# Tile 1's gated outputs in two banks, with the state products in half rows of the array

## What is computed

```python
    q_dec = q * jnp.exp(b)
    k_inv = k * jnp.exp(-b)
    a = jnp.where(causal, jnp.einsum('bhncd,bhnsd->bhncs', q_dec, k_inv), 0.0)
    o_intra = jnp.einsum('bhncs,bhnsv->bhncv', a, v)
    ...
    o_inter = jnp.einsum('bhncd,bhndv->bhncv', q_dec, s_prev)
    return (o_intra + o_inter).reshape(B, H, S, dv)
    ...
    o_gla = rms_norm(o_gla.transpose(0, 2, 1, 3), gla_out_gain[l])
    o_gla = (o_gla * jax.nn.silu(gr.reshape(...))).reshape(B, S, GLA_V)
```

## Time and profile before

| what | value |
|---|---|
| median of 3 runs | 301.67 us (301.47 to 302.24) |
| the profiled execution | 301.75 us, of which the span from first to last instruction is 300.0 us |
| mean granted clock of TensorE | 0.996 of full speed |
| PE busy | 292.4 us (97%) |
| DVE busy | 242.4 us (81%) |
| ACT busy | 171.6 us (57%) |
| DMA | 55.45 MB, mean 185 GB/s |

### The profile page before, as it was taken

One profiled execution on the slowest core, in us unless ns is written; L12 is line 12 of the kernel. 1 busy time (PEld: TensorE's weight loads), 2 busy tenths in 40 slices (PEclk: granted clock), 3 DMA queues, 4 the chain that ended last, 5 costly groups with the idle time before them and its releaser, 6 DMA issues.

```text
span 300.0 us, 4026 instructions
## 1 busy us (share of the span) xinstructions
PE 292.4 (97%) x1373; PEld 243.3 (81%) x1373; DVE 242.4 (81%) x403; ACT 171.6 (57%) x242; POOL 19.1 (6%) x41
## 2 busy tenths in 40 slices
PE   7999999999999999999999999999999999999992
PEld 7788888788898888887888888888888888888881
DVE  1999999977879687988888888889897978787155
ACT  2898999969765897717170808080808080813123
POOL 5050100000021001300000000000000000000011
PEclk9999999999999999999999999999999999999998
DMA  7987836737867121392929292929291929030003
GB/s 235 364 289 266 263 119 251 218 131 264 298 190 227 53 92 70 95 329 90 331 82 336 79 343 69 346 66 352 63 363 47 367 54 366 25 120 0 0 0 140
DMA packets 37318, 55.45 MB, mean 185 GB/s; under 512 B 2950, under 2 KB 26554, under 8 KB 37306
## 3 DMA queue, kind: packets, MB, share of 16 engines
q1 hardware_dynamic: 37140, 55.13, 54.4%
q10 hardware_dynamic: 166, 0.17, 0.2%
HBM read 53.72 MB, written 1.57 MB: 184 GB/s over the span
## 4 chain that ended last, share of the span: by engine, by line
PE 94%; DMA 2%; DVE 1%; issue 1%; POOL 1%; ACT 0%; SPq 0%; POOLq 0%; DVEq 0%
PE acc L508 15%; PE acc L510 15%; PE acc L509 15%; PE aux L508 13%; PE aux L509 13%; PE aux L510 13%; DMA raw<-in_w_in 2%; PE aux L613 1%; PE acc L562 1%; PE acc L565 1%; PE acc L568 1%; PE aux L683 1%; DVE x_sb L1366 1%; PE aux L707 1%; PE aux L665 1%
## 5 line engine op out<-in xcount | busy, mean ns | idle before, releaser
L1137 DVE TENSOR_TENSOR w_lo<-raw,w_hi 128x2048 fp32r<-128x2048 f32 x47 | 105.6, 2286 | 14.5 <-ACT w_hi L877 14.4
L877 ACT CAST w_hi<-raw 128x2048 fp32r<-128x2048 f32 x47 | 87.9, 1908 | 4.4 <-DMA raw<-in_w_ffn_up 2.1
L508 PE MATMUL aux<-w_hi,aT_hi 128*128 128x512 f32 (+1 forms) x180 | 69.8, 388 | 0.0
L509 PE MATMUL aux<-w_lo,aT_hi 128*128 128x512 f32 (+1 forms) x180 | 69.7, 387 | 0.0
L510 PE MATMUL aux<-w_hi,aT_lo 128*128 128x512 f32 (+1 forms) x180 | 69.7, 387 | 0.0
L1432 DVE STREAM_TRANSPOSE reuse_c<-reuse_c 32x128 f32<-32x128 f32 x160 | 48.4, 303 | 2.4
L1080 ACT CAST pT_hi<-reuse_c 128x512 fp32r<-128x512 f32 x10 | 6.2, 621 | 72.9 <-DVE reuse_c L1432 72.9
L508 PE MATMUL acc<-w_hi,aT_hi 128*128 128x512 f32 x118 | 47.1, 399 | 0.0
L510 PE MATMUL acc<-w_hi,aT_lo 128*128 128x512 f32 x118 | 46.1, 390 | 0.0
L509 PE MATMUL acc<-w_lo,aT_hi 128*128 128x512 f32 x118 | 46.0, 390 | 0.0
L508 PEld LDWEIGHTS aux<-w_hi,aT_hi 128*128 128x128 f32 x180 | 33.8, 188 | 6.9
(11 more groups left out here) (203 smaller groups left out, 285.0 us busy)
## 6 DMA issues: line engine op xcount, KB each, us to landing
raw<-in_w_ffn_gate SPq DMA_DIRECT2D x22, 512.0 KB, 4.3
raw<-in_w_ffn_up SPq DMA_DIRECT2D x22, 512.0 KB, 5.4
raw<-in_w_ffn_down SPq DMA_DIRECT2D x22, 512.0 KB, 6.0
raw<-in_w_in SPq DMA_DIRECT2D x20, 512.0 KB, 4.8
raw<-in_w_out SPq DMA_DIRECT2D x8, 512.0 KB, 4.3
raw<-in_w_in SPq DMA_DIRECT2D x8, 256.0 KB, 6.2
x_sb<-in_x SPq DMA_DIRECT2D x2, 512.0 KB, 3.7
m_moves<-reuse_c SPq DMA_DIRECT2D x1, 512.0 KB, 2.7
```

The costliest lines, as they stand in the source:

```text
L508: nc.tensor.matmul(dst, left_hi[:, k, tok], right_hi, start=first, stop=False)
L509: nc.tensor.matmul(dst, left_hi[:, k, tok], right_lo, start=False, stop=False)
L877: nc.scalar.copy(w_hi[:, slot % RING, :], raw[:, slot % RAW, :]).then_inc(hi_ready, 1)
L1137: nc.vector.tensor_tensor(w_lo[:, slot % RING, :], raw[:, slot % RAW, :], w_hi[:, slot % RING, :].bitcast(f32), ALU.subtract).then_inc(lo_ ...
```

## The change

Tile 1's outputs go to two banks: the even heads stay in aux bank 2, the odd heads go to acc bank 1. For each pair of heads PE first multiplies both heads' scores with the values, then both state products, each over the 64 rows of its own head. Since acc bank 1 is also the target of out_product (0, 0, 1), group 0's order becomes (0,0), (1,0), (0,1), (1,1), with a wait on a new semaphore ahead of the third, which DVE raises once it has normalized tile 1's odd heads. ACT squares tile 1 in two instructions, DVE normalizes it in two.

```diff
+        gla_late = (aux[:, 2, :], acc[:, 1, :])
...
+        gla_taken = sem("gla_taken")
...
-                for t in range(T):
-                    for h in range(HEADS):
+                for h in range(HEADS):
+                    cols = slice(h * DV, (h + 1) * DV)
+                    last = nc.tensor.matmul(aux[:, 1, cols], a_gla[:, 0, h, :], gv[:, 0, cols], start=True, stop=True)
+                last.then_inc(gla_in_psum, 1)
+                for pair in range(PAIRS):
+                    for h in (2 * pair, 2 * pair + 1):
                         cols = slice(h * DV, (h + 1) * DV)
-                        last = nc.tensor.matmul(aux[:, 1 + t, cols], a_gla[:, t, h, :], gv[:, t, cols],
-                                                start=True, stop=t == 0)
-                        if t:
-                            last = nc.tensor.matmul(aux[:, 1 + t, cols], glaT[:, 4 * PAIRS + h // 2, :], state[:, h, :],
-                                                    start=False, stop=True)
-                    last.then_inc(gla_in_psum, 1)
+                        nc.tensor.matmul(gla_late[h % 2][:, cols], a_gla[:, 1, h, :], gv[:, 1, cols], start=True, stop=False)
+                    for h in (2 * pair, 2 * pair + 1):
+                        cols, rows = slice(h * DV, (h + 1) * DV), slice(h % 2 * DK, (h % 2 + 1) * DK)
+                        last = nc.tensor.matmul(gla_late[h % 2][:, cols], glaT[rows, 4 * PAIRS + pair, :], state[rows, h, :],
+                                                start=False, stop=True)
+                last.then_inc(gla_in_psum, 1)
...
-                for n in range(2):
-                    if t == 0 and n == 0:
-                        unit_ready(IN_UNITS + 1)
-                    out_product(t, 0, n)
+                if t == 0:
+                    unit_ready(IN_UNITS + 1)
+                out_product(t, 0, 0)
+            pe.wait_ge(gla_taken, 1)
+            for t in range(T):
+                out_product(t, 0, 1)
...
-            for t in range(T):
-                act.wait_ge(gla_in_psum, t + 1)
-                nc.scalar.activation(squares[:, t * W:(t + 1) * W], aux[:, 1 + t, :], ACT.Square).then_inc(sq_ready, 1)
+            act.wait_ge(gla_in_psum, 1)
+            nc.scalar.activation(squares[:, 0:W], aux[:, 1, :], ACT.Square).then_inc(sq_ready, 1)
+            act.wait_ge(gla_in_psum, 2)
+            for par, bank in enumerate(gla_late):
+                dst, src = (v.rearrange("p (a e v) -> p a e v", a=PAIRS, e=2)[:, :, par, :] for v in (squares[:, W:2 * W], bank))
+                last = nc.scalar.activation(dst, src, ACT.Square)
+            last.then_inc(sq_ready, 1)
...
+            def normed_late(par):
+                dst = o_gla[:, 1, par:HEADS:2, :]
+                factor = rstd_h[:, 1, HEADS + par:2 * HEADS:2].unsqueeze(2).to_broadcast([P, PAIRS, DV])
+                src = gla_late[par].rearrange("p (h v) -> p h v", h=HEADS)[:, par:HEADS:2, :]
+                return nc.vector.tensor_tensor(dst, src, factor, ALU.mult)
+
+            normed_late(1).then_inc(gla_taken, 1)
             normed(1, 0, 1, o_gla[:, 0, :, :])
-            then(normed(1, 1, 2, o_gla[:, 1, :, :]))
+            then(normed_late(0))
```

## The result

The changed kernel takes 302.62 us in the median of 22 runs, the kernel before 302.10 us in 22 runs beside them. One of the changed kernel's runs took 603.75 us and is left out of the ratio. The ratio is 1.0018, with a 95% interval of 1.0011 to 1.0025: 0.33 to 0.76 us slower, so by less than 0.3%, but measurably. The profiled execution took 302.1 us, its span 300.2 us, at a granted clock of 0.997. The forecast was 302.0 us, no difference of 0.3%.

What follows compares the result with a forecast made beforehand. TensorE (PE), busy for 97% of the span, was taken as the bound. Two trips of 0.40 us less 0.45 us saved by pairing gave +0.35 on the median 301.67, so 302.0 us; range 301.2 to 302.8 us.

Steps and rivals of the forecast that it cites:

- PE is the bound and its time reaches the end: Whole kernel: each nanosecond added to or taken off PE reaches the end, unless another engine's lateness makes a third wait.
- A trip costs 0.34 to 0.40 us, and the two together +0.23 to +0.35: gla_outputs: going into half rows and back loses 0.34 to 0.40 us, saves 0.22; two such trips, +0.35 us taken.
- The halves overlap: gla_outputs: even and odd heads' state products run in pairs, 8 passes in 4 steps, 0.45 us saved.
- the rival without overlap: State products: the halves take turns, no step is saved, both trips are paid; +0.80 us, 302.5 us; chance 0.08.
- the rival with a trip for each change of half: State products: moving between heads' rows also drains, four trips paid, no step saved; +1.6 us, 303.3 us; chance 0.04.
- Trips cost nothing: Rival, gla_outputs: changing between full and half rows is free, so all 0.45 us are gained; 301.2 us; chance 0.08.
- ACT and DVE are 0.35 to 0.5 us later, with room: Behind gla_outputs: split Squares start DVE's reduction 0.35 to 0.5 us later; PE's later points keep 0.6 to 2.8 us room.
- The reordering is what covers the wait: Group 0's out_products: the new order gives the gla_taken wait 2.8 us of room, the old order 0.1 us.
- The size: Whole kernel: +0.35 us, median 302.0 us, called no difference because 0.3% (0.9 us) was the least a measurement could tell.

Runs made afterwards that it cites:

- r1: The kernel before, with tile 1's products of gla_outputs issued nine times instead of once; 316.61 us, ratio 1.0476 to the kernel before.
- r2: The changed kernel, with tile 1's products of gla_outputs issued nine times instead of once; 319.99 us, ratio 1.0595 to the kernel before.
- e4: The changed kernel with odd heads' state products over all 128 rows, only even heads' in half rows; 303.27 us, before 302.22.
- e2: The changed kernel with all four state products together, between the scores-and-values products of heads 0, 1 and heads 2, 3; 302.35 us, before 302.22.
- e5: The changed kernel with all four state products together, issued in head order 0, 2, 1, 3; 302.42 us, before 302.22.
- e3: The changed kernel with group 0's out_products in the old order, the wait ahead of the second; 302.73 us, before 302.10.
- e7: The changed kernel with group 0's old out_product order and DVE normalizing the odd heads last of three; 303.32 us, before 301.99.
- e6: The changed kernel with state products together in head order 0, 2, 1, 3, plus six discarded extras each for heads 2 and 3; 305.43 us, one run.

## Why the prediction was right, point by point

- *PE is the bound and its time reaches the end.* Right: r1 added 14.3 us of PE work and 14.5 us came out. This point covers the span; the time outside it is not in the prediction.
- *A trip costs 0.34 to 0.40 us, and the two together +0.23 to +0.35.* Right: 0.39 and 0.35 in the changed kernel, 0.39 in r2; the stretch grew by 0.29, of it 0.23 up to the transposes, where I had expected 0.1 to 0.2. I took the upper end, from L650. The second trip was cheaper; it leads into transposes, whose weight loads last 0.14 us instead of 0.19, but that this is the reason is not shown. That changing the tiling mode drains the engine, as the Trainium skill has it in TensorEngine Tiling (Array Packing), Key Properties, agrees with e4, where a trip without any pair costs the same, 0.77 us for two.
- *The halves overlap.* Right: pairs 0.01 us apart or less. That a sum is added to a bank just written did not keep them apart, so the rival without overlap falls, and the rival with a trip for each change of half too. The time alone would not have shown it: 302.62 is nearer to the 302.5 of no overlap than to the 302.0 of the forecast. The starts do, and the stretch: without overlap it would be that of e4, 4.56 us, and it is 4.08.
- *Trips cost nothing.* Wrong as a rival, shown by e4 and r2. The speedup of up to two that the Trainium skill gives in TensorEngine Tiling (Array Packing), Theoretical Speedup, is there within the pair (two passes a step in the changed kernel, e2 and e5). With only two steps saved in a trip, 0.22 us, the trip takes more than that gives, 0.39.
- *ACT and DVE are 0.35 to 0.5 us later, with room.* Right in kind, too dear: counted from the start of gla_outputs, the reduction began 3.72 us after it instead of 3.51, +0.21. Two Squares of 0.38 us start 0.28 apart, so together they last 0.66 and not 0.8 to 0.94.
- *The reordering is what covers the wait.* Wrong, without effect on the time: I gave it 0.1 us of room in the old order, since I added all the worst cases; e3 shows no wait. DVE taking the odd heads first is enough to cover it, and without either the wait is there, as e7 shows.
- *The size.* Too small. The measured time lies 0.62 us above the 302.0 of the forecast, and inside the range because that was drawn wide, past no overlap, up to 302.8. Of the 0.62, 0.43 is the base: the kernel before itself came to 302.10 in 22 runs, where the sum started from 301.67 in three. Against before it is +0.52 instead of +0.35: the trips give +0.29, and the 0.23 us outside the span make the rest. The sum has no term for time outside the span. The nine-fold form agrees: 3.4 by medians, 3.1 by spans. And 0.3% was not the least that can be told: 22 runs told 0.18% from nothing.

## What to carry to other kernels

Products in the two halves of the rows, side by side, double the rate, but only within a trip. Each trip costs a price at its two ends, here 0.39 us (0.35 where it led into transposes), or three and a half steps of 0.112. So gather all products of one shape into one trip before splitting: two trips that saved two steps each lost time, and one trip that saved four just broke even on PE. A wait on another engine can be covered by what that engine does first, without a new order on the engine that waits.

## What the runs showed of the hardware

TensorE does not start its products in the order of issue when they sit in different halves of the rows: in e5 and e6 the first pass of the upper half overtook three passes (one and a half fp32 products) of the lower half. In e6, with eight products ahead, it came no earlier than beside the 13th of 16 passes. So that nothing reorders the program, as is said of the kernel before, holds for the instruction lists and not for the starts on TensorE.
